# Rotary query projections of two heads in one group, and neighbouring rows of the down weights on one partition

## What is computed

```
z = rmsnorm(x, g_mix) @ w_in            # feeds two branches
qk, v_m, o_m, i_pre, f_pre, c_q, c_kv, k_r, g_a, g_b = split(z)
# branch A: mLSTM recurrence in chunks of 64 tokens, 4 heads
# branch B: latent attention, 8 heads
q = (rmsnorm(c_q, g_q) @ w_uq).reshape(B, T, 8, 128 + 64)
q_rope = rope(q[..., 128:], pos)        # x*cos + swapped(x)*sin, 64 wide
q_lat  = q[..., :128] with w_uk
s = (q_lat . lat + q_rope . kr) * scale ; softmax ; @ lat ; w_uv
x = x + (sigmoid(g_a)*y_a + sigmoid(g_b)*y_b) @ w_out
# mixture of experts: top 4 of 32
gu  = xb @ w_gu[e] + b_gu[e]            # 1024 x 2048
hid = (up + 1) * gate * sigmoid(1.702 * gate)
y   = hid @ w_dn[e] + b_dn[e]           # 1024 x 1024
```

## Time and profile before

| | |
|---|---|
| time, median of 3 runs | 1734.08 us (1733.89 to 1734.19) |
| the profiled execution's own time | 1737.26 us |
| its span, first to last instruction | 1735.4 us |
| mean granted TensorE clock | 0.941 of full speed |
| PE busy | 1558.7 us |
| DVE, ACT, POOL busy | 361.6, 361.4, 122.1 us |
| moved by DMA | 477.35 MB, mean 275 GB/s |

### The profile page before, as it was taken

The page is one execution under the profiler, slowest core; times in us unless marked ns, Lnnn a source line. Parts: engine busy times, 40 slices in busy tenths (PEclk is TensorE's granted clock), DMA queues, the critical chain, the costliest instruction groups (busy, mean ns, idle before and its releaser), DMA issues.

```text
span 1735.4 us, 20567 instructions
## 1 busy us (share of the span) xinstructions
PE 1558.7 (90%) x7116; PEld 705.7 (41%) x7117; DVE 361.6 (21%) x871; ACT 361.4 (21%) x685; POOL 122.1 (7%) x219
## 2 busy tenths in 40 slices
PE   6999999989999989878889997887999887998994
PEld 4566666556666443222223332222333222332331
DVE  3644532233321241010101101010101101011015
ACT  3444342444410111110111111110111111111111
POOL 0100000000000000000001100000101000001010
PEclk9989999899999989998989998898999998999996
DMA  7212113121274349999989999999899999769897
GB/s 252 79 49 76 49 49 121 50 83 39 97 241 157 149 155 355 408 412 414 405 352 371 352 410 411 415 411 409 318 402 347 407 411 406 279 248 409 330 407 264
DMA packets 108777, 477.35 MB, mean 275 GB/s; under 512 B 12995, under 2 KB 16944, under 8 KB 75970
## 3 DMA queue, kind: packets, MB, share of 16 engines
q1 hardware_dynamic: 100696, 461.76, 68.2%
q0 software_dynamic: 7808, 15.00, 2.6%
q10 hardware_dynamic: 234, 0.08, 0.0%
HBM read 471.25 MB, written 15.50 MB: 280 GB/s over the span
## 4 chain that ended last, share of the span: by engine, by line
PE 70%; DMA 18%; DVE 5%; issue 3%; SPq 2%; ACT 1%; DVEq 0%; POOL 0%; ACTq 0%; POOLq 0%
PE bank L607 27%; PE bank L1015 21%; DMA ring<-in_w_gate_up 16%; PE bank L1038 16%; PE bank L611 3%; PE bank L1021 1%; DVE r_kv L1412 1%; DVE r_v L1415 1%; DMA b_router_b<-in_b_router 1%; PE bank L865 1%; DVE r_qk L1409 0%; SPq L561 0%; SPq L568 0%; DVE r_c L1415 0%; SPq L477 0%
## 5 line engine op out<-in xcount | busy, mean ns | idle before, releaser
L1015 PE MATMUL bank<-ring,r_kv 128*64 128x512 f32 x2184 | 521.6, 625 | 91.0 <-DMA ring<-in_w_gate_up 91.0
L1015 PEld LDWEIGHTS bank<-ring,r_kv 128*64 128x64 f32 x2184 | 157.1, 142 | 404.3 <-issue 309.2
L1038 PE MATMUL bank<-ring,r_kv 128*64 128x512 f32 x1248 | 296.1, 619 | 0.7 <-ACT r_kv L1108 0.7
L607 PE MATMUL bank<-r_xt,ring 128*128 128x336 f32 x848 | 255.1, 456 | 1.9 <-DVE r_xt L1412 1.5
L1409 DVE TENSOR_SCALAR r_kv<-bank 128x512 f32<-128x512 f32 (+1 forms) x80 | 55.0, 687 | 926.3 <-PE bank L1021 921.0
L607 PEld LDWEIGHTS bank<-r_xt,ring 128*128 128x128 f32 x848 | 161.1, 193 | 82.5 <-issue 11.8
L1038 PEld LDWEIGHTS bank<-ring,r_kv 128*64 128x64 f32 x1248 | 94.4, 146 | 201.6 <-issue 200.5
L1108 ACT ACTIVATE r_xt<-bank 128x512 f32<-128x512 f32 x39 | 23.3, 597 | 518.0 <-PE bank L1038 518.0
L1355 ACT ACTIVATE r_o<-r_kv 128x512 f32<-128x512 f32 x39 | 24.6, 632 | 323.7 <-DVE r_kv L1409 323.7
L611 PEld LDWEIGHTS bank<-const,r_v 64*128 64x128 f32 (+3 forms) x524 | 45.2, 138 | 82.2 <-DVE r_v L1415 48.6
L607 PE MATMUL bank<-ring 128*128 128x336 f32 (+2 forms) x288 | 73.1, 439 | 4.7 <-ACT ring L1190 3.7
(11 more groups left out here) (241 smaller groups left out, 950.4 us busy)
## 6 DMA issues: line engine op xcount, KB each, us to landing
ring<-in_w_gate_up SPq DMA_DIRECT2D x256, 1024.0 KB, 18.0
ring<-in_w_down SPq DMA_DIRECT2D x128, 1024.0 KB, 14.8
ring<-in_w_in SPq DMA_DIRECT2D x12, 2048.0 KB, 7.7
ring<-in_w_proj_b SPq DMA_DIRECT2D x2, 2048.0 KB, 8.4
ring<-in_w_proj_a SPq DMA_DIRECT2D x2, 2048.0 KB, 10.2
ring<-in_w_out SPq DMA_DIRECT2D x2, 2048.0 KB, 7.9
ring<-y_rows SPq DMA_DIRECT2D x8, 512.0 KB, 9.7
ring<-in_w_uq SPq DMA_DIRECT2D x2, 1152.0 KB, 8.9
```

The source lines that it names most:

```text
L607: ins = pe.matmul(out, l, r, start=(n == 0), stop=(n == len(pairs) - 1), **kw)
L1015: ins = pe.matmul(half(gate_bank if q < 2 else up_bank, q % 2), xg[:, k, :], w[:, 512 * q:512 * q + 512], start=False, stop=False, skip_gr ...
L1038: ins = pe.matmul(half(out_bank, t), hidT[:, j, BLK * h:BLK * h + BLK], w[:, h, 512 * t:512 * t + 512], start=(j == 0 and h == 0), stop=(j ...
```

## The change

Two edits.

Rotary projections: for a pair of heads, the `qr` projections of both heads are one job in one bank, head 0 in the partitions 0 to 63 and head 1 in 64 to 127, their matmuls taking turns. The normed rotary query `qx`, the product with the sine `qtmp` and the constants `cos`, `sin` and `swap` have 128 partitions; `swap` is block diagonal, so that `qrs` is one job with one matmul. DVE evicts once, multiplies by sine once and by cosine once; the six adds into `qr` stay, and three of them read partitions 64 to 127 and write 0 to 63. The list has eight jobs fewer, the constants 64 columns more.

Down weights: tile `j` holds the rows `256 j + 2 p + s` with s = 0 and 1 on partition p, which is 8 KB in one piece. `hidden_turned` takes every other column of `hid` for each of its four transposes, and `down` uses half `h = j // 2`.

The recurrence is not touched by the diff.

```diff
-                  ("cos", NT), ("sin", NT), ("swap", 64),
+                  ("cos", NT), ("sin", NT), ("swap", 128),
...
-        for h in (0, 1):
-            j += [("qn", hp, h), ("qr", hp, h)]
+        j += [("qn", hp, h) for h in (0, 1)] + [("qr", hp)]
...
-        j += [mla_fill(hp, "q")] + [("qrs", hp, h) for h in (0, 1)] + [("ql", hp, i) for i in range(4)]
+        j += [mla_fill(hp, "q")] + [("qrs", hp)] + [("ql", hp, i) for i in range(4)]
...
-        dn = i["w_down"][0].rearrange("e (h j p) f -> p e h j f", p=128, h=2)
+        dn = i["w_down"][0].rearrange("e (j p s) f -> p e j (s f)", p=128, s=2)
...
                     project(("qn", hp, h), w, at, 128, cq, 3)
-                    project(("qr", hp, h), w, at + 128, 64, cq, 3)
+                b = begin("qr", hp)
+                for k in range(3):
+                    for h in (0, 1):
+                        at = 192 * (2 * (hp % 2) + h) + 128
+                        ins = pe.matmul(b[64 * h:64 * h + 64, 0:NT], PV[w][:, k, at:at + 64], cq[:, k, :], start=(k == 0),
+                                        stop=(k == 2), skip_group_check=True)
+                end(ins, "qr", hp)
...
-                for h in (0, 1):
-                    taken(pe, "qr", hp, h)
-                    b = begin("qrs", hp, h)
-                    end(group(b[0:64, 0:NT], [(cst("swap", 64), qx[:, h, :])]), "qrs", hp, h)
+                taken(pe, "qr", hp)
+                b = begin("qrs", hp)
+                end(group(b[:, 0:NT], [(cst("swap"), qx)]), "qrs", hp)
...
-                for j in range(4):
-                    ins = turn(ht_bank[:, 128 * j:128 * j + 128], hid[:, 128 * j:128 * j + 128])
+                for j in range(2):
+                    for s in range(2):
+                        at = 128 * (2 * j + s)
+                        ins = turn(ht_bank[:, at:at + 128], hid[:, 256 * j + s:256 * j + 256:2])
...
-                for h in range(2):
+                h = j // 2
+                for s in range(2):
                     for t in range(2):
-                        ins = pe.matmul(half(out_bank, t), hidT[:, j, BLK * h:BLK * h + BLK],
-                                        w[:, h, 512 * t:512 * t + 512], start=(j == 0 and h == 0),
-                                        stop=(j == 3 and h == 1), skip_group_check=True)
+                        ins = pe.matmul(half(out_bank, t), hidT[:, 2 * (j % 2) + s, BLK * h:BLK * h + BLK],
+                                        w[:, s, 512 * t:512 * t + 512], start=(j == 0 and s == 0),
+                                        stop=(j == 3 and s == 1), skip_group_check=True)
```

More of the change, by code:

```diff
@@ L44 @@
 _at = 0
-for _name, _n in [("ident", 128), ("ones", 128), ("below", 128), ("cos", NT), ("sin", NT), ("swap", 64),
+for _name, _n in [("ident", 128), ("ones", 128), ("below", 128), ("cos", NT), ("sin", NT), ("swap", 128),
                   ("mask", NT), ("sel", 4 * 128), ("expert", NE), ("block", NB1), ("lane", 1),
@@ L510, in _ @@
             panel("v1")
-            filled(sp, "qr", 3, 1)
+            filled(sp, "qr", 3)
             panel("g2")
@@ L663, in _ @@
             b = begin("krs")
-            end(group(b[0:64, 0:NT], [(cst("swap", 64), kr_raw)]), "krs")
+            end(group(b[0:64, 0:NT], [(cst("swap", 64)[:, 0:64], kr_raw)]), "krs")
             def fill(name):
@@ L1534, in _ @@
                     take(tt(qn[:, h, :], bank(("qn", hp, h))[:, 0:NT], rq, ALU.mult), "qn", hp, h)
-                    filled(dve, "qr", hp, h)
-                    take(tt(qx[:, h, :], bank(("qr", hp, h))[0:64, 0:NT], rq[0:64, :], ALU.mult), "qr", hp, h)
+                filled(dve, "qr", hp)
+                take(tt(qx, bank(("qr", hp))[:, 0:NT], rq, ALU.mult), "qr", hp)
                 if hp == 0:
@@ L1539, in _ @@
                 fill(mla_fill(hp, "q"))
+                filled(dve, "qrs", hp)
+                take(tt(qtmp, bank(("qrs", hp))[:, 0:NT], cst("sin"), ALU.mult), "qrs", hp)
+                step(tt(qx, qx, cst("cos"), ALU.mult))
                 for h in (0, 1):
-                    filled(dve, "qrs", hp, h)
-                    take(tt(qtmp, bank(("qrs", hp, h))[0:64, 0:NT], cst("sin", 64), ALU.mult), "qrs", hp, h)
-                    step(tt(qx[:, h, :], qx[:, h, :], cst("cos", 64), ALU.mult))
-                    for j, ((dst, a), (_, b)) in enumerate(zip(by_chunk(qr, h, qx[:, h, :]), by_chunk(qr, h, qtmp))):
+                    rows = slice(64 * h, 64 * h + 64)
+                    for j, ((dst, a), (_, b)) in enumerate(zip(by_chunk(qr, h, qx[rows, :]),
+                                                               by_chunk(qr, h, qtmp[rows, :]))):
                         ins = tt(dst, a, b, ALU.add)
```

20 lines of the change are left out of this document (10 added, 10 removed).

## The result

| | median us | runs | lowest to highest | mean granted clock |
|---|---|---|---|---|
| kernel before, beside it | 1734.13 | 4 | 1733.89 to 1735.47 | |
| changed kernel | 1713.24 | 4 | 1704.34 to 1714.92 | 0.948 |
| changed kernel, timed again | 1715.46 | 6 | 1710.80 to 1717.01 | 0.945 |
| changed kernel, a third time | 1715.77 | 6 | 1709.55 to 1716.70 | 0.945 |

The first timing gives a ratio of 0.9873, 95% interval [0.9852, 0.9895]: 20.9 us less, where 16.7 were forecast. The two later ones, with 11 and 16 runs of the kernel before beside them, give 0.9895 [0.9872, 0.9918] and 0.9884 [0.9863, 0.9904]. All 16 runs of the changed kernel together have a median of 1715.1 us. The direction and the larger part of the size are as forecast; the rest of this text is about the difference. One run of the kernel before, of 3155 us, lies far from all its others and is left out everywhere.

A forecast was written before the change was run, and what follows sets the result against it. PE was taken to bound 70% of the span and DMA 18%, with 17 of 39 blocks ending on a transfer. The terms -9.9 - 6.9 + 0.1 = -16.7 us gave a median of 1717.4 us, range 1713 to 1725.

The forecast's parts named there:

- the rotary term: Attention on PE: paired rotary projections save 1.84 us and the swap 0.64 per pair of heads, 9.9 us for four pairs.
- the strided loads: PE's transposes of hid in the experts: every-other-column loads cost at most 26 ns more each, 2.3 us; taken as 0.
- The transfer of the down tiles: Expert weights: 8 KB pieces raise 410 to 423.5 GB/s, 0.33 us less in each of 21 sets, 6.9 us.
- Rival (c): Transposes of hid: strided weight loads take 371 ns or more instead of 141, making the kernel slower; chance 0.04.
- the best case: Rotary projections: second half wholly hidden and the switch of shapes free, 4 x 2.6 = 10.4 us less.
- Eight jobs fewer leave every later job in its old bank: PE's job list: dropping eight jobs doesn't move later jobs to other banks; no time counted.
- The constants: Start of the kernel: 64 more columns load ahead of b_router_b, for which DVE waits; 0.1 us charged.
- Cover and waits: DVE's last add stays about 3.8 us ahead of the scores; 17 waits for transfers, or 16, remain.
- (a): Expert down tiles: their rate does not move, since time or buffer place sets it; 1724.3 us, chance 0.10.
- (b): Attention: PE's gain is not passed on, through DVE, ACT or lost overlap; 1727.3 us, chance 0.09 in whole or part.
- (d): Stretches' starts: up tiles queued earlier fill DMA engines sooner, plus the upper ends of terms; 1713 us, chance 0.04.
- (e): The change doesn't do all its name says: the recurrence stands as it did, worth 0, included in the forecast.

The follow-up runs named there:

- e8: Changed kernel with each down tile still one contiguous megabyte but in 4 KB pieces, transposes reading adjacent columns: median 1717.52 us, ratio 0.9910.
- e2: Kernel before with the down-weight half of the change alone: median 1729.86 us, ratio 0.9973.
- e3: Kernel before with only the transposes of the hidden rows reading every other column, down weights in their old places: median 1732.37 us, ratio 0.9990.
- e7: Changed kernel with DVE writing hid reordered, so that PE's transposes read adjacent columns: median 1711.77 us, ratio 0.9879.
- e4: Kernel before with only the new layout of the down tiles, transposes from adjacent columns as before: median 1726.00 us, ratio 0.9962.
- e16: Kernel before with a pair's four projections ordered plain, plain, rotary, rotary and nothing paired: median 1729.01 us, ratio 0.9982.
- e6: Changed kernel with 20 more wait instructions, fulfilled at once, in DVE's stream ahead of its loop over blocks: median 1715.21 us, ratio 0.9912.
- e13: Kernel before with 44 more wait instructions, fulfilled at once, in DVE's stream ahead of its loop over blocks: median 1736.21 us, ratio 1.0011.
- e17: Kernel before with 44 more wait instructions placed where DVE waits for PE anyway, ahead of its loop over blocks: median 1732.53 us, ratio 0.9994.
- e14: Kernel before with the two rotary projections of a pair of heads paired, but two swaps of 64 rows each: median 1725.33 us, ratio 0.9951.
- e15: Kernel before with one swap of 128 rows for a pair of heads, projections not paired: median 1727.19 us, ratio 0.9974.

## Why the prediction was right or wrong

**The step that failed** is the rotary term. It was added up as 1.84 + 0.64 = 2.48 us a pair, 9.9 us in all, with nothing for what PE loses in the old form at each change between 128 and 64 columns. The runs show 2.94 us in each of the four pairs, 11.8 us. A second bound failed as well, that of the strided loads (26 ns at most, 67 measured). The rest of the way to the 20.9 us of the first timing is, by the regression, the clock of its four runs.

**The transfer of the down tiles, 6.9 us: right in cause, at the upper end in size.** The stretches moved from 409 to 422 GB/s, and e8 shows that the pieces did it. In the profiled executions the layout gives 6.9 us (before to e2, e3 to e2), 5.1 (e8 to e7) and 3.8 (before to e4), and 6.4 ± 1.4 over all seventeen; the timings give 4.5 (e3 to e2) and 4.4 (e4) at equal clock. The term was counted as if all of the 21 sets' time ran at the clean rate. What is certain is 4 to 7 us; what takes the rest where it is less stays open. A part may be the correction itself: TensorE has the lower clock for 132.3 us of the experts' part before, 132.1 in e3, 125.3 in e2, and if those 7 us come from the edit, the regression takes some 2.4 us too much away (half of 7 us is 0.002 of the mean clock).

**The strided loads, taken as 0: wrong.** What failed here is the bound from the earlier trace rows. I took the load of 8 columns for the nearest case and 0.66 ns a column as the most. Measured is (208 - 83) / 128 = 0.98 ns. A load of 8 columns is nearly all fixed cost, and a slope can't be read from it. In time they cost 0.09 us a block, since the four overlap, or 1.6 us in the 18 blocks bound by PE (e3), and the transfer blocks of e3 are 1.6 us shorter: the sum is unchanged. The timing of e3 can't tell either, 1.8 us less by the medians and 1.4 ± 0.7 more at equal clock. So the 0 came out by luck. The prediction let every block bound by PE pass its time on to the end, and that is not what the traces show. The Trainium skill, "Advanced Engine Details and Errata", section "SBUF Cachelines", asks for two hits on a line of 16 B, and a step of 8 B gives two; the measurement of 208 against 141 ns decides, and here the rule doesn't describe weight loads of float32. Rival (c) needed 371 ns and did not come.

**The rotary half, 9.9 us: right in mechanism, too small.** The halves run side by side as the earlier trace rows said. The term left out that PE loses time when the width of its matmuls changes; e16 shows 0.35 us of that in the projections of a pair. The paired projections give 2.04 us instead of 1.84: those 0.35, and 1.69 for the second rotary group, which is nearly hidden. The rest is in the swap (0.71 instead of 0.64), the latent query behind it (0.11) and the filler ahead (0.08). 4 x 2.94 = 11.8 us. The 10.4 that I gave as the best case assumed that the change of shapes cost nothing *in the new form*; that it cost something in the old one was not looked for, though the earlier trace rows held it: 24 records in 7.37 us there, against 16 in 4.71 for the filler behind them, 0.307 us a record against 0.294.

**"Eight jobs fewer leave every later job in its old bank": true, and not all.** Twenty instructions fewer moved DVE's loop in its stream, and its step to PE became 0.116 us shorter in each of 39 blocks (e6, e13, e17). No part of the prediction looked at instructions that the diff doesn't touch. It is worth some 2 us in the blocks bound by PE and about 1 us or less in the whole.

**The constants, 0.1 us: not seen.** DVE's wait for `b_router_b` ends at 30.21 us before. In the first profile of the changed kernel it ends at 30.52 and the chain behind it starts 0.66 us later, which the sum of 18.6 took as a cost. But in the other two it ends at 30.27 and 30.18, with the chain starting 0.56 us later and 0.02 sooner than before. In e2 and e4, whose constants are those of before, it ends at 30.39 and 30.54, with the chain 1.73 and 0.84 us later. So the 0.66 us are the run's, not the constants', and no run shows the 0.1.

**Cover and waits: right.** DVE ends 3.6 us ahead of the scores (3.8 forecast), 17 waits for transfers remain, no new wait appeared. SP's issue is no shorter, as assumed in the sum.

**The rivals.** (a), no gain from pieces: refuted by e2 and e8. The Trainium skill, "DMA: Bandwidth & Descriptors", section "Specifications", gives 512 B as the smallest transfer for line rate; here pieces of 4 KB stay 3% below those of 8 KB (410 against 422 GB/s), and the measurement decides. (b), attention's gain not passed on: refuted. (d), more than forecast: it is what was measured first, but not by its mechanism; the excess is from the rotary part and the clock. (e) held.

**The sum.** At equal clock the change is worth 17.2 ± 0.6 us against 16.7. That is closer than its terms, and so in part luck: the rotary half gave 13.3 for 9.8, the down half 3.1 for 6.9. By the traces it is 11.8 and 6.4, 18.2 us; the 1 us between that and 17.2 stays open. The remaining difference to the 20.9 us of the first timing is the clock of its runs, which the forecast took as that of before.

## What to carry to other kernels

Ask of each group of small matmuls how often it changes shape against its neighbours, before asking how many there are: to order them by width gave 0.35 us a pair here in the trace, and to put them on opposite halves hid a whole group. Look also at instructions that the diff doesn't touch, for an edit that removes instructions ahead of a loop moves the loop. Don't add a gain in blocks bound by PE to the whole where other blocks wait for a queue of transfers: here those took most of it back. And where two runs of one kernel differ by more than the effect, count in the trace, and set the medians beside the granted clock of their runs.

## What the runs showed of the hardware that was not expected

- A load of 128 float32 columns as weights takes 141 ns if they are adjacent, and 208 if they are every other one; VectorE reads every other column in the same 0.69 us (e7).
- The rate of a full set of DMA engines is 417 to 425 GB/s with 8 KB pieces. With 4 KB it is 409 to 411, whether the tile is one region or two (before, e8).
- Matmuls on opposite partition and column halves overlap even as separate groups into different banks (e14: two of 64 rows in 0.72 us instead of 1.27).
- The loop's place in VectorE's instruction stream decides 0.11 us of a dependency inside it. Twenty instructions fewer, or 44 more, take it away, and 20 fewer and 20 more bring it back. 8 and 12 fewer (e14, e15) take it away too, so a shift of 8 is enough.
